# Expert stage of a hybrid decoder step: rounds of 128 slots in fp32 column groups instead of one expert of 96 slots in three fp32r passes

## The reference

```python
lg = xt @ router_group;  g_sel = argmax(lg);  p_sel = softmax(lg)[g_sel]
le_sel = (xt @ router_expert).reshape(-1, 4, 8)[g_sel]
top_p, top_i = top_k(softmax(le_sel), 2);  top_p /= top_p.sum()
comb = sum(one_hot(g_sel * 8 + top_i) * top_p) * p_sel
for e in range(32):
    y += comb[:, e] * ((silu(xt @ w_gate[e]) * (xt @ w_up[e])) @ w_down[e])
out = rmsnorm(h + y) * norm_final            # prompt rows and sample rows
```

## Time and profile before

| what | value |
|---|---|
| median of 3 runs | 1011.46 us |
| the profiled execution's own time | 1011.97 us |
| its span, first to last instruction | 1010.1 us |
| PE busy | 917.7 us, 91% of the span |
| DVE busy | 595.2 us, 59% |
| ACT busy | 503.5 us, 50% |
| POOL busy | 234.6 us, 23% |
| first gather of the expert stage issued | 650.36 us |
| last down matmuls of the last experts in the chain | 931.7 us |

### The profile page before, as it was taken

The page is one execution under the profiler, slowest core; times in us unless marked ns, Lnnn a source line. Parts: engine busy times, 40 slices in busy tenths (PEclk is TensorE's granted clock), DMA queues, the critical chain, the costliest instruction groups (busy, mean ns, idle before and its releaser), DMA issues. The chain is left out here.

```text
span 1010.1 us, 13905 instructions
## 1 busy us (share of the span) xinstructions
PE 917.7 (91%) x4971; PEld 725.2 (72%) x4971; DVE 595.2 (59%) x1051; ACT 503.5 (50%) x870; POOL 234.6 (23%) x304
## 2 busy tenths in 40 slices
PE   3899999999999999987899999499999999999962
PEld 3799887888878887775678776377777777777621
DVE  4503533253324432366685336888999999888756
ACT  4523344334443434334332212568888888888614
POOL 1102223233213322202452201211011011010435
PEclk9999999999999999998699999689999999999977
DMA  8032221321232122317145534999999999999976
GB/s 250 38 109 77 89 73 52 96 78 58 74 114 72 54 74 75 120 32 226 64 138 180 177 125 180 358 314 385 388 394 394 398 398 393 400 401 373 350 276 229
DMA packets 88363, 203.92 MB, mean 202 GB/s; under 512 B 11903, under 2 KB 55231, under 8 KB 76006
## 3 DMA queue, kind: packets, MB, share of 16 engines
q1 hardware_dynamic: 77806, 169.99, 47.4%
q0 software_dynamic: 5984, 17.18, 5.1%
q10 hardware_dynamic: 4504, 15.85, 4.1%
HBM read 167.02 MB, written 39.99 MB: 205 GB/s over the span
## 5 line engine op out<-in xcount | busy, mean ns | idle before, releaser
L1017 PE MATMUL pj<-n_hi,w_hi 128*128 128x350 f32 (+1 forms) x576 | 199.2, 346 | 3.5 <-DVE n_lo L1337 3.5
L1017 PE MATMUL pj<-n_lo,w_hi 128*128 128x350 f32 (+1 forms) x576 | 188.5, 327 | 0.0
L1017 PE MATMUL pj<-n_hi,w_lo 128*128 128x350 f32 (+1 forms) x576 | 187.6, 326 | 0.0
L1941 DVE TENSOR_TENSOR e_lo<-e_raw,e_hig 128x2048 fp32r<-128x2048 f32 x64 | 145.9, 2282 | 0.0
L1017 PEld LDWEIGHTS pj<-n_hi,w_hi 128*128 128x128 f32 x576 | 109.9, 191 | 35.4 <-issue 33.6
L1299 DVE CUSTOM_DVE_ANT_0 sc<-pj,strip 128x512 f32<-128x512 f32 (+5 forms) x120 | 60.9, 544 | 119.0 <-PE pj L1083 78.0
L1937 ACT ACTIVATE e_hig<-e_raw 128x2048 fp32r<-128x2048 f32 x64 | 122.5, 1918 | 10.3 <-DMA e_raw<-in_w_up 9.6
L1017 PEld LDWEIGHTS pj<-n_lo,w_hi 128*128 128x128 f32 x576 | 110.2, 191 | 0.6
L1017 PEld LDWEIGHTS pj<-n_hi,w_lo 128*128 128x128 f32 x576 | 109.8, 191 | 0.9 <-issue 0.8
L1989 PE MATMUL pj<-e_hig,xT_hi 128*96 128x512 f32 x256 | 104.8, 410 | 0.0
L1989 PE MATMUL pj<-e_hig,xT_lo 128*96 128x512 f32 x256 | 101.3, 396 | 0.0
(11 more groups left out here) (291 smaller groups left out, 1637.5 us busy)
## 6 DMA issues: line engine op xcount, KB each, us to landing
e_raw<-in_w_up SPq DMA_DIRECT2D x32, 1024.0 KB, 16.7
e_raw<-in_w_gate SPq DMA_DIRECT2D x32, 1024.0 KB, 20.7
e_raw<-in_w_down SPq DMA_DIRECT2D x32, 1024.0 KB, 21.2
w_raw<-in_w_in SPq DMA_DIRECT2D x24, 512.0 KB, 4.0
expert_rows<-yo ACTq DMA_DIRECT2D x32, 384.0 KB, 8.1
expert_rows<-logits SPq DMA_DIRECT2D x26, 384.0 KB, 4.6
wo_raw<-in_w_out SPq DMA_DIRECT2D x8, 512.0 KB, 5.2
k_page<-in_cache_k SPq DMA_DIRECT2D x16, 256.0 KB
```

Of the source, the lines that this page charges most:

```text
L1017: ins = pe.matmul(pj[g % 2][:, 0:tn], ws[w][:, P * k:P * (k + 1)], x[:, k, t0:t0 + tn], start=(m == 0), stop=(m == 23))
L1941: eng.tensor_tensor(e_lo[r][:, q, :], e_raw[r][:, q, :], e_hi(par, q).bitcast(F32), ALU.subtract).then_inc(s_lo[q], 1)
```

## The change

- A round is 128 slots. The 32 x 96 slots are laid end to end, so there are `NRD` = 24 rounds. 32 slots are a column group, an expert has three of them, and a round has four. In `pieces`, two neighbouring groups of one expert that begin at an even group are one piece of 64 columns, any other group is a piece of 32. So of every three rounds the first has pieces of 64, 32, 32, the second 64, 64, the third 32, 32, 64.
- The matmuls are plain fp32 from `e_raw`. The `high` and `low` operations and their tiles are gone. Each piece is a matmul of its own, with its expert's weights, into its own rows of the bank.
- The ring of weights has 5 slots. The gate and up pieces of the fourth and fifth experts are issued ahead of the wait for the first gather, their down pieces behind it.
- `expert_rows` is gone, and with it the 26 stores of zeros to it in the first part, the store of `yo` and the whole final part. Instead POOL gathers the residual rows of each round (`gather_h`). DVE adds the gated result to them (`dve_z`). Where it is the token's first expert in the order of rounds, POOL scatters the row back to `h_dram` (`scatter_back`). Where it is the second, ACT, POOL and DVE norm it (`act_square`, `root`, `dve_out`) and POOL scatters it to the outputs (`scatter_out`, two scatters). An index past the end drops a row. The gather of round r waits for the scatter of round r-2.
- The routing makes more tables: rank to slot in the round (`homes`, `route_place`), and a second table with "is this the last one" and the gate by slot (`gates`, `place_pay`, `tables`, with 18 plain fp32 matmuls in `pe_r`). The gates are computed ahead of the stage and not in its 24th turn.
- The extra blocks do the same by slot row.

The core of the diff:

```diff
+NRD = NE * CB // P
-                if 1 <= s <= MAXB - FIRSTS:
-                    sp.dma_start(y_dram...[:, FIRSTS + s - 1:FIRSTS + s]..., zero_row ...).then_inc(s_fill, 16)
...
+            dve.wait_ge(s_step, did.n[0])
+            did(dve.tensor_tensor(high, rk0[:, :, t0:t1], two(far[:, t0:t1], T), ALU.is_ge))
+            did(dve.tensor_tensor(at_p, rk0[:, :, t0:t1], two(home[:, t0:t1], T), ALU.add))
+            did(dve.tensor_scalar(past, rk0[:, :, t0:t1], float(CB), float(GONE), ALU.is_ge, ALU.mult))
...
+            tokens(dve, did, P, pj[1][:, 0:NRD], NRD, 0, s_step)
             dve.sem_inc(s_slots, 1)
+            gates(dve, did)
...
+            dve.wait_ge(s_pm, 2)
+            tables(dve, did, P, pj[3][:, 0:NRD], pj[3][:, NRD:2 * NRD], NRD, 0, s_step)
+            dve.sem_inc(s_slots, 1)
...
+            for c in range(2):
+                pe.wait_ge(s_ph, 4 + c + 1)
+                for t in range(NT):
+                    ins = pe.matmul(pj[3][:, 0:2 * NRD], place_hot[:, c, t, :].bitcast(F32), place_pay[:, c, t, :, :]...)
...
-        RD = 4
+        RD = 5
...
+        def pieces(r):
+            runs, q = [], 0
+            while q < 4:
+                n = (4 * r + q) // 3
+                size = 2 if q % 2 == 0 and (4 * r + q + 1) // 3 == n else 1
+                runs.append((n, 32 * q, 32 * (q + size)))
+                q += size
+            return runs
...
+        def gather_h(pool, r):
+            if r >= 2:
+                pool.wait_ge(s_back[r % 2], 16 * (r // 2))
+            if r >= 3:
+                pool.wait_ge(s_z, 2 * (r - 3) + 2)
+            gather(pool, hy[r % 3][:], h_dram, tab[:, r, 0:1], s_hy[r % 3])
+
+        def scatter_back(pool, r):
+            pool.wait_ge(s_z, 2 * r + 2)
+            scatter(pool, h_dram, TOK, tab[:, r, 1:2], zs[r % 2][:], s_back[r % 2])
...
             for k in range(k0, k1):
-                for a, (x, w) in enumerate(((xT_hi, e_hig[par]), (xT_hi, e_lo[r]), (xT_lo, e_hig[par]))):
-                    ins = pe.matmul(gu_bank[par][0:CB, :]..., x[:, par, k, :], w[:, 0:2, FF * k:FF * (k + 1)], ...)
+                for n, a, b in pieces(r):
+                    ins = pe.matmul(gu_bank[r % 2][a:b, :].rearrange("p (q f) -> p q f", q=2), xT[:, r % 2, k, a:b],
+                                    e_raw[n % RD][:, 0:2, FF * k:FF * (k + 1)], start=(k == 0), stop=(k == KC - 1))
...
+            for b in range(2):
+                if r >= 1:
+                    pe.wait_ge(s_z, 2 * (r - 1) + b + 1)
+                for f in range(2):
+                    for n, p0, p1 in pieces(r):
+                        o = D * f + 512 * b
+                        ins = pe.matmul(dn[b][p0:p1, :], hT[:, f, p0:p1], e_raw[n % RD][:, 2, o:o + 512], start=(f == 0), stop=(f == 1))
+                ins.then_inc(s_dn, 1)
...
+        def dve_z(dve, r):
+            dve.wait_ge(s_hy[r % 3], 16 * (r // 3 + 1))
+            if r >= 2:
+                dve.wait_ge(s_back[r % 2], 16 * (r // 2))
+            for b in range(2):
+                dve.wait_ge(s_dn, 2 * r + b + 1)
+                part = slice(512 * b, 512 * (b + 1))
+                dve.scalar_tensor_tensor(zs[r % 2][:, part], dn[b][:], gate_s[:, r:r + 1], hy[r % 3][:, part], ALU.mult, ALU.add).then_inc(s_z, 1)
...
         def sp_m(sp):
             sp.wait_ge(s_dm, 2 * NT)
             for q in (1, 0, 2):
-                load_piece(sp, 2, q, 2, 0, 2)
-            load_piece(sp, 3, 1, 3, 0, 3)
+                load_expert(sp, 2, q)
+            for q in (1, 0):
+                load_expert(sp, 3, q)
+            sp.wait_ge(s_csl, 2 * NT)
+            for q in (1, 0):
+                load_expert(sp, 4, q)
             sp.wait_ge(s_lge, NT)
             sp.wait_ge(s_hsq, NT)
             sp.wait_ge(s_xg[0], 16)
-            for q in (0, 2):
-                load_piece(sp, 3, q, 3, 0, 3)
+            load_expert(sp, 3, 2)
+            load_expert(sp, 4, 2)
...
+            for n in range(NRD + 2):
+                if n + 3 < NRD:
+                    gather_x(pool, n + 3)
+                if n >= 2:
+                    scatter_back(pool, n - 2)
+                if n - 2 >= DONE0:
+                    pool.wait_ge(s_sq, n - 2 - DONE0 + 1)
+                    root(pool, did, n % 2, s_pool)
+                    scatter_out(pool, n - 2)
+                if 2 <= n < NRD:
+                    gather_h(pool, n)
...
+            for n in range(NRD + 1):
+                if n - 2 >= DONE0:
+                    dve_out(dve, n - 2)
+                if n < NRD:
+                    dve_mult(dve, n)
+                if n >= 1:
+                    dve_z(dve, n - 1)
+                if 2 <= n < 10:
+                    route_more(dve, did, (0, 1, 2, 3, 4, 5, 8, 10)[n - 2])
```

More of the change, by code:

```diff
@@ new lines, in tokens, with do, tables @@
+        def tokens(dve, did, M, found, n, n0, counted):
+            def do(ins):
+                did(ins)
+                dve.wait_ge(counted, did.n[0])
+            sf = slot_f[0:M, n0:n0 + n]
+            do(dve.tensor_scalar(sf, found, 0.0, float(GONE), ALU.is_equal, ALU.mult))
+            do(dve.scalar_tensor_tensor(sf, found, -1.0, sf, ALU.add, ALU.add))
+            do(dve.tensor_copy(tab[0:M, n0:n0 + n, 0], sf))
+        def tables(dve, did, M, last, gate, n, n0, counted):
+            def do(ins):
+                did(ins)
+                dve.wait_ge(counted, did.n[0])
+            sf = slot_f[0:M, n0:n0 + n]
+            notl, idx, low, row = ((tmp_t if n0 == 0 else tmp_x)[0:M, i, :] for i in range(4))
+            did(dve.tensor_copy(gate_s[0:M, n0:n0 + n], gate))
+            did(dve.scalar_tensor_tensor(idx, last, float(GONE), sf, ALU.mult, ALU.add))
+            do(dve.tensor_scalar(notl, last, -float(GONE), float(GONE), ALU.mult, ALU.add))
+            did(dve.tensor_copy(tab[0:M, n0:n0 + n, 1], idx))
+            do(dve.tensor_tensor(notl, notl, sf, ALU.add))
+            for i, first in ((2, META), (3, PROMPT)):
+                do(dve.tensor_scalar(low, sf, float(first), 2.0 * GONE, ALU.is_lt, ALU.mult))
+                do(dve.scalar_tensor_tensor(row, notl, -float(first), low, ALU.add, ALU.add))
+                do(dve.tensor_copy(tab[0:M, n0:n0 + n, i], row))
@@ L1957, in pe_xt, with experts_of, first_round, last_round @@
-        def pe_xt(pe, n, r):
-            pe.wait_ge(s_xg[r], 16 * turn(n))
-            rows = xg[r][0:CB, :].rearrange("s (p k) -> s k p", k=KC)
+        DONE0 = NG * CB // P
+        BACKS = [len(range(w, NRD, 2)) for w in range(2)]
+        OUTS = [len([r for r in range(w, NRD, 2) if r >= DONE0]) for w in range(2)]
+        def experts_of(r):
+            return sorted({(4 * r + q) // 3 for q in range(4)})
+        def first_round(n):
+            return 3 * n // 4
+        def last_round(n):
+            return (3 * n + 2) // 4
@@ new lines, in act_xt, with pe_gu @@
+                if r >= 2 and q == 0:
+                    act.wait_ge(s_gu, r - 1)
+                act.activation(xT[:, r % 2, 4 * q:4 * q + 4, :].rearrange("p c t -> p (c t)"), xb[q][:], ACT.Copy).then_inc(s_xte, 1)
+        def pe_gu(pe, r, k0, k1):
+            if k0 == 0:
+                pe.wait_ge(s_xte, 2 * r + 2)
+                for n in entering(r):
+                    for q in range(2):
+                        pe.wait_ge(s_er[3 * (n % RD) + q], 16 * (n // RD + 1))
+                if r >= 2:
+                    pe.wait_ge(s_hh, r - 1)
@@ new lines, in pool_m @@
+            for r in range(3):
+                gather_x(pool, r)
+            for r in range(2):
+                gather_h(pool, r)
+            pool.wait_ge(s_slots, 2)
+            for n in range(NRD + 2):
[9 more added lines that the diff above has]
+                    gather_h(pool, n)
```

807 lines of the change are left out of this document (312 added, 495 removed).

## The result

| | kernel before | changed kernel |
|---|---|---|
| median of the runs side by side | 1010.35 us (1009.11 to 1011.9, 4 runs) | 1173.69 us (1173.02 to 1177.04, 4 runs) |
| span of the profiled execution | 1010.1 us | 1171.2 us |
| PE busy | 917.7 us, 91% | 1093.8 us, 93% |
| DVE busy | 595.2 us | 382.2 us |

The changed kernel is slower: ratio 1.162, 95% interval 1.159 to 1.165. The forecast was 979 us, with 1184 us for the second rival, the one in which pieces of 64 and of 32 columns exclude each other. That rival is what happened.

A forecast was written before the change was run, and what follows sets the result against it. PE sets the pace with DMA just behind; both limits hold in turn. Last down at 964 (DMA's 961 plus 3), end 13, span 977, plus 1.9 outside the span: 979 us, range 963 to 1190.

The forecast's parts named there:

- the second rival: Expert rounds on PE: pieces of 64 and 32 columns exclude each other, 1.98 us a step, 1184 us; chance 0.30.
- I take 0.865: One PE step (one k of gate and up, or half of down): 0.865 us whatever the number of pieces; upper bound 1.98.
- The residual loop: Add, scatter, landing, gather, landing: 21.3 us for two rounds of 24.2, so hidden by 3 us.
- the first rival: Expert rounds on PE: pieces run side by side, 979 us, own range 966 to 1005; chance 0.54.
- The third rival: Residual rows in the expert stage: landings of 12.9 us make 14.7 us a round, 1032 us; chance 0.10.
- The start: First gate and up on PE, after routing and list matmuls: begins at about 664, bounds 660 and 667.
- The round of equal widths: One expert round on PE, 128 slots: twelve steps, entries and transposes sum to 12.1 us.
- The bytes: Rows gathered and scattered after the change: 25.8 MB, or 1.07 MB a round; empty slots move nothing.
- The full DMA rate: DMA engines in the expert stage: 395 GB/s, between 386 and 398.
- The end: From the last down through add, norm, two scatters and landing: 13 us, bounds 10 and 18.
- DVE's 14 us at 816.90: PE's wait for busy DVE in the kernel before, some 14 us net: claimed to go, the routing fitting into a round.
- The early loads: Two extra weight pieces ahead of the first gather: worth at most 5 us of a queue at nine tenths.

The follow-up runs named there:

- the version of one width: Changed kernel with every column group a piece of its own, so all pieces are 32 columns wide: 1010.47 us, ratio 0.9998 to the kernel before.
- the grouped widths: Changed kernel with, inside each stretch, all pieces of 64 first and then all of 32: 1149.63 us, ratio 1.1398 to the kernel before.
- without the loop: Changed kernel with all pieces 32 wide, the second gather reading `normed` and waiting for no scatter: 994.39 us, ratio 0.9837 to the kernel before.

## Why the prediction was wrong

**The step that failed** is "I take 0.865", for pieces of unequal width beside each other. Measured: 1.98 us. The prediction had this number as the other bound; the choice between the bounds was wrong. The range of 963 to 1190 holds the measured 1173.7 only because it took in the second rival. The way was forecast wrong: 0.54 stood on faster. The argument was that in the rows where a change of shape empties the array, both shapes use the same columns. That was absence of evidence: no row showed disjoint columns of unequal width, and every change of width that the trace did show cost something. With one value for all rows that I had, "a change of shape empties the array", the second rival would have been the likelier. The rule of the Trainium skill (TensorEngine Tiling (Array Packing), section Key Properties) is that a change of the tiling mode, and not only of the tile, drains the engine. The loads of 760.30 to 763.26 agree with it, and so do both runs on it, the one width at 1010.5 us and the grouped widths at 1149.6.

**The residual loop** is a second error, hidden in the changed kernel and visible in the version of one width. The loop of 21.3 us was set against two rounds of 24.2, as if scatters and gathers of odd and even rounds went on beside each other. The prediction named what is queued on POOL behind the waiting gather (the next rows) but not the next scatter, which belongs to the loop. And the landings were taken at 8.9 us, while the scatters took 11.9 to 14.3 once the DMA engines were full. So the first rival's number, 979 us, was wrong for its own case too: side by side gives 1010.5 us. The third rival had the loop, but as two landings of 12.9 us in two rounds, at 1032 us. What the runs show is one landing in each round, by POOL's order, 13.7 us a round on average.

**Terms that held.** The start: 664 against 665.11, in part by luck. The list matmuls were 0.22 us each and not 0.17 (7.92 us for 36, where the sum had 6.2), but they began at 653.66, a microsecond earlier than the sum had it. The clock was the same in both rows, 0.50, which is the level of 1.2 GHz. What differs is the weight load: PE's weight loads are busy for 7.76 of the 7.92 us, 0.216 each with 128 columns, and in the row of before 2.31 of 2.42, 0.165 each with 96 columns. The prediction took the row's price over to one-hots that are a third wider. The round of equal widths: 12.1 us, measured 12.1. The step of equal widths, four pieces in the time of one, also with 64, 64. The bytes: 25.8 MB of rows. The full DMA rate: 386 to 398 GB/s assumed, 416 and 393 seen without the loop. The end: 13 us, measured 12.6, but with two errors against each other: the issue of the last scatter began 8.0 us after the last matmul instead of 5.8, and 4.6 us remained from there instead of 7.2. DVE's 14 us at 816.90 are gone, and no wait for routing takes their place. The second rival's sum: 1184 against 1173.7. Most of the missing 1.4 us in three rounds is one down product of 6.97 us instead of 7.8 (797.52 in the chain). There gate and up end with two 32s in the upper columns, and the down product of the round before begins with two 32s in the lower ones. Their weights are loaded at once, so equal widths overlap in the changed kernel too:

```profile
796.48 0.11 PEld L2083 LDWEIGHTS pj<-e_raw,hT 128*32 128x32 f32 x2
796.49 0.12 PEld L2041 LDWEIGHTS pj<-e_raw,xT 128*32 128x32 f32 x2
```

**The early loads**: worth at most 5 us, I wrote; measured nothing in the version of one width, and 0.5% to the bad side when one of them alone is added to the kernel before.

**What stays open.** Without the loop the median is 15 us above the 979 of the sum, while the profiled execution is within 4 us of it. The late gathers are read from that one profile, the fastest of six executions; that they account for the other 12 us is not shown, and no run shows what would make them land in time. Nor does a run show an order on POOL in which the residual gather waits neither for a scatter just issued nor for the add before it.

## What to carry to other kernels

Before splitting PE's columns among experts, make every piece the same width. If a ragged one is unavoidable, split the wide ones: four streams of 32 took the time of one, while a stream of 64 next to streams of 32 doubled the step and made the whole kernel 16% slower. When a DMA loop (store, land, read back) shares an in-order queue with other work, list all that stands behind each wait, and look for the next store of the same loop among it; where no row shows two things side by side, give the bound that assumes they exclude each other its full chance.

## What the runs showed that was not expected

- A busy share can't show this loss. In the stage PE was busy 491.14 of 493.00 us, while in two of three rounds only half of its columns worked at a time. The idle time of the weight loads in sum is no clear sign either: for L2041 it was 218.8 us here and still 99.7 us in the version of one width. The single gap tells them apart: 0.81 to 0.84 us before each load where the width changes, 0.30 where it doesn't.
- Gathers took longer to land where the DMA engines were fuller. The residual gathers' median was 4.1 us in the changed kernel, with a DMA share of 0.59 in the stage, and 8.3 us in the version of one width, where the share was 0.87 to 1.01 from 700 to 950. Single ones took 17.09, 21.14 and 23.11 us. The medians of before were 6.2 to 12.9 us.
- One weight piece of 1 MiB ahead of the first gather made its landing 9.70 us in place of 5.66.
